# Moving a small side computation and its transfers from the projection part of a gated-DeltaNet stage into its matrix-inverse part

## The reference, cut to what matters

```
shift, scale, gate = split(c @ w_ada + b_ada, 3)          # modulate: w_ada is 1024 x 3072
h = x * (1 + scale) + shift

# gated_delta_rule, per head and chunk
lower = where(strict, (k*beta) @ k.T * decay, 0)
sol   = triangular_solve(lower + I, [v*beta | k*beta*exp(gc)])   # u and w
step:  v_new = u - w @ state;  o = qg @ state + qk @ v_new;  state = state*gl + kdec.T @ v_new
```

## Time and profile before

| | |
|---|---|
| median of 3 executions | 2713.7 us (2710.06 to 2719.28) |
| profiled execution, time | 2713.7 us |
| profiled execution, span of its instructions | 2711.8 us |
| mean granted TensorE clock | 0.971 of full |
| TensorE busy over the span | 93% |
| VectorE busy over the span | 37% |
| GpSimd busy over the span | 12% |
| `delta_stage` | about 1478 to 1940 us, turns of some 109 us |

### The profile page before, as it was taken

One profiled execution on the slowest core, in us unless ns is written; L12 is line 12 of the kernel. 1 busy time (PEld: TensorE's weight loads), 2 busy tenths in 40 slices (PEclk: granted clock), 3 DMA queues, 4 the chain that ended last, 5 costly groups with the idle time before them and its releaser, 6 DMA issues. The chain is left out here.

```text
span 2711.8 us, 37865 instructions
## 1 busy us (share of the span) xinstructions
PE 2525.0 (93%) x13849; PEld 1377.0 (51%) x13850; DVE 1005.6 (37%) x2302; ACT 672.4 (25%) x1468; POOL 337.3 (12%) x390
## 2 busy tenths in 40 slices
PE   6999999999999999999996999999899999899995
PEld 2665656656764443333332476685774434333332
DVE  2444344433543322322207535446343332222217
ACT  1031030310312222222222433443312222222221
POOL 0101001010001111111100212122101111111110
PEclk9999999999999999999997999999999999999998
DMA  7624326252628999999965211312437999999966
GB/s 281 191 63 146 102 92 189 61 164 66 224 101 322 365 421 420 411 413 413 407 250 215 78 50 59 97 54 66 163 131 290 345 420 420 399 414 411 404 264 276
DMA packets 177815, 654.93 MB, mean 242 GB/s; under 512 B 26884, under 2 KB 88684, under 8 KB 122504
## 3 DMA queue, kind: packets, MB, share of 16 engines
q1 hardware_dynamic: 112752, 394.89, 37.4%
q10 hardware_dynamic: 29784, 149.13, 14.4%
q0 software_dynamic: 35136, 109.10, 11.5%
HBM read 614.18 MB, written 53.52 MB: 246 GB/s over the span
## 5 line engine op out<-in xcount | busy, mean ns | idle before, releaser
L1462 DVE TENSOR_SCALAR core_oT<-moe_tx,moe_by,moe_plus 128x128 f32<-128x128 f32 x360 | 123.0, 404 | 661.6 <-PE moe_tx L1709 661.4
L675 PE MATMUL attn_proj<-core_hT,core_ring 128*128 128x512 f32 x768 | 334.4, 596 | 8.5 <-ACTq L497 5.1
L1734 PE MATMUL moe_ph<-weights_w,core_oT 128*32 128x512 f32 (+2 forms) x1216 | 307.4, 615 | 8.8 <-issue 8.7
L1748 PE MATMUL moe_py<-weights_w,moe_hT 128*32 128x512 f32 (+2 forms) x1296 | 312.8, 596 | 0.9 <-ACT moe_hT L1186 0.9
L1734 PE MATMUL moe_pr<-weights_w,core_oT 128*64 128x512 f32 (+2 forms) x864 | 276.6, 604 | 10.7 <-issue 9.7
L675 PEld LDWEIGHTS attn_proj<-core_hT,core_ring 128*128 128x128 f32 x768 | 146.5, 191 | 188.9 <-issue 183.2
L2392 PE MATMUL gdn_pj<-core_hT,core_ring 128*128 128x512 f32 x512 | 226.8, 597 | 0.0
L1269 POOL DMA_INDIRECT y_rows<-moe_ysb,moe_yidx x90 | 93.6, 1040 | 951.2 <-ACT moe_ysb L1199 726.1
L1186 ACT COPY moe_hT<-moe_th 128x256 f32<-128x256 f32 x90 | 33.6, 374 | 659.2 <-PE moe_th L1697 659.2
L671 PE MATMUL attn_proj<-core_ring,core_hT 128*128 128x256 f32 x768 | 176.5, 391 | 0.0
L671 PEld LDWEIGHTS attn_proj<-core_ring,core_hT 128*128 128x128 f32 x768 | 169.3, 282 | 11.2 <-issue 3.8
(11 more groups left out here) (410 smaller groups left out, 3433.6 us busy)
## 6 DMA issues: line engine op xcount, KB each, us to landing
weights_w<-in_expert_w_dram SPq DMA_DIRECT2D x160, 1024.0 KB
weights_w<-in_expert_w_dram ACTq DMA_DIRECT2D x92, 1024.0 KB
core_ring<-in_expert_w_dram SPq DMA_DIRECT2D x54, 1024.0 KB
core_hT<-in_expert_w_dram SPq DMA_DIRECT2D x48, 1024.0 KB
core_ring<-in_attn_w_in_dram SPq DMA_DIRECT2D x36, 1024.0 KB, 7.4
weights_w<-y_rows SPq DMA_DIRECT2D x32, 1024.0 KB, 13.1
core_ring<-in_expert_w_dram ACTq DMA_DIRECT2D x30, 1024.0 KB
attn_ada_w<-in_ada_w_dram POOLq DMA_DIRECT2D x64, 384.0 KB, 5.8
```

The costliest lines, as they stand in the source:

```text
L675: last = nc.tensor.matmul(proj[n % 2][:], w[:, j % SLOTS, kk, half_ * P:(half_ + 1) * P], c.hT[:, kk, :], start=kk == 0, stop=kk == KT - 1)
L1462: last = nc.vector.tensor_scalar(xT[:, b, k], tx[1][:, k - 4], by[:, k:k + 1], plus[:, k:k + 1], ALU.mult, ALU.add)
L1734: last = nc.tensor.matmul(ph[p % 2][at, :], xT[:, p % 2, k, at], w13[ew.up_place(n)[0]][:, :, k], start=k == 0, stop=k == KT - 1)
L1748: last = nc.tensor.matmul(py[n][at, :], hT2[:, p % 2, k, at], w2[ew.down_place(m)[0]][:, k, half(n)], start=k == 0, stop=k == 1)
```

## The change

Loads 2 to 5 are taken out of the early part of GpSimd's list and put behind the two products that make P0 (`P_ready`), ahead of the link matrices. Loads 6 and 7 are put between the link matrices of s = 0 and those of s = 1. All eight adds are taken out of the early part of VectorE's list. Adds 0 and 1 are put behind the E additions of step 0, adds 2 and 3 behind those of step 1, adds 4 and 5 behind step 2, adds 6 and 7 behind step 3. Numbers, sizes and buffers are as before.

```diff
@@ GpSimd's list
                 for h in range(HP):
-                    ada.load(pool, i, 2 + h)
                     pool.wait_ge(silu_ready, NCONV * i + h + 3)
                     pool.tensor_tensor(E1[h][:], kT[h][:], kT[h][:], ALU.mult).then_inc(kk_sq, 1)
                 for h in range(HP):
-                    ada.load(pool, i, 4 + h)
...
                 for h in range(HP):
-                    ada.load(pool, i, 6 + h)
...
                     pool.tensor_tensor(P0[h][:], M[h][:], over_t(masks[:, BELOW]), ALU.mult).then_inc(P_ready, 1)
+                for j in range(2, 6):
+                    ada.load(pool, i, j)
                 for s, dst in enumerate((P0, P1, P0)):
                     for h in range(HP):
...
                         pool.tensor_tensor(dst[h][:], M[h][:], over_t(masks[:, LINK + s]), ALU.mult).then_inc(n_ready[s], 1)
+                    if s == 0:
+                        ada.load(pool, i, 6), ada.load(pool, i, 7)
@@ VectorE's list
-                conv(0, K_), ada.add(dve, i, 0), conv(1, K_), ada.add(dve, i, 1), mask_causal(0), mask_causal(1)
-                conv(2, Q_), ada.add(dve, i, 2), conv(3, Q_), ada.add(dve, i, 3), conv(4, V_), ada.add(dve, i, 4)
-                norm_k(0), norm_k(1), ada.add(dve, i, 5), norm_q(0), norm_q(1)
-                keys(0), ada.add(dve, i, 6), keys(1), conv(5, V_), ada.add(dve, i, 7)
+                conv(0, K_), conv(1, K_), mask_causal(0), mask_causal(1)
+                conv(2, Q_), conv(3, Q_), conv(4, V_)
+                norm_k(0), norm_k(1), norm_q(0), norm_q(1)
+                keys(0), keys(1), conv(5, V_)
...
                         nc.vector.tensor_tensor(dst[h][:], ps[h][0][:], src[h][:], ALU.add).then_inc(e_ready[s], 1)
+                    if s < 4:
+                        ada.add(dve, i, 2 * s), ada.add(dve, i, 2 * s + 1)
```

## The result

The changed kernel takes 2744.18 us (median of 4, 2739.17 to 2751.66) against 2711.88 us (median of 4, 2706.49 to 2719.28): a ratio of 1.011, 95% interval 1.0086 to 1.0134. It is slower, by some 30 us. The forecast was 2739 us, range 2728 to 2752.

The account below looks back on a forecast made before the run. TensorE, busy for 93% of the span, was taken as the bound, with nil slack at step 2's E addition. Terms 3.0 + 1.55 + 0.7 + 1.1 = 6.3 us a turn, 25 over four turns: 2713.7 + 25 = 2739 us, range 2728 to 2752.

Parts of the forecast that it names:

- Nothing comes back from the projections: Projections: TensorE never waits for VectorE's adds there, so removing 7.7 us of them a turn gains 0 us.
- The E addition of step 2, 3.0 us: Inverse, head 0: adds 2 and 3 wait for slices ahead of this E addition, making TensorE's transpose 3.0 us late.
- GpSimd's queue, 1.55 us more: Inverse: loads 2 to 5 stand ahead of the first link matrices, adding 1.55 us, 4.55 us late in all.
- The third stall, 0.7 us for the link matrix behind load 7: Second link: loads 6 and 7 stand ahead of its link matrices, so TensorE waits 0.7 us more.
- The clock, 1.1 us net: Inverse: TensorE's gaps lower the granted clock, costing 1.1 us net a turn, between 0 and 2.6.
- Contention, left in the range: Inverse: adds 4 and 5 can overlap GpSimd's link matrices, delaying loads 6 and 7 by up to 0.6 us; not summed.
- adds 6 and 7 end by 1705.3: hidden: Inverse, after step 3: these adds end before the next E addition is wanted at 1706, so they cost nothing.
- The sum: Whole loop: 3.0 + 1.55 + 0.7 + 1.1 = 6.3 us a turn, 25 us over four turns.
- A: Inverse: the adds fit into VectorE's idle time, no change, 2713.7 to 2721 us; 1.7 us delay if slices had landed; chance 0.06.
- B: Projections: relief from the adds makes the kernel faster, at most 4 x 0.3 = 1.2 us; chance of real gain 0.02.
- C: Inverse: clock takes 2.6 us, with later landings and contention a turn costs 10.2 us, 2754 us; chance 0.17 for over 2746.

Follow-up runs that it names:

- the filled kernel: Changed kernel with five unread 128x512 products a turn added to TensorE, four before the E addition of step 2, one before the first link matrix: 117.45 us a turn, ratio 1.0126.
- only the second half was moved: Against the kernel before, only adds 4 to 7 and loads 6 and 7 moved to the change's places: 112.29 us a turn, ratio 1.0039.
- the four-buffer kernel with small link products: Changed kernel with four slice buffers, loads 2 and 3 early, and GpSimd's six link products a turn cut to one column: 110.73 us a turn, ratio 1.0014.
- the first experiment: Kernel before with the arithmetic of seven of a turn's eight adds left out, waits and counting kept: 109.09 us a turn, ratio 0.9999.
- the four-buffer kernel: Changed kernel with four slice buffers instead of two and loads 2 and 3 early in GpSimd's list: 115.74 us a turn, ratio 1.0103.

## Why the prediction was right, and where its terms were off

**Nothing comes back from the projections.** Right, and shown: windows of 62.0 us after, and 109.09 us a turn with the arithmetic of the adds gone.

**The E addition of step 2, 3.0 us.** Right in mechanism; it measured 3.6. The short term was the landing of the second slice of a pair. I took 3.4 us for every slice; load 2, issued at 1814.51, landed after 3.5 us, but load 3, issued 1.1 us later, after 4.2. The trace of the kernel before had this already: its loads 0 and 1 go out as a pair, and the second lands after 3.9 to 4.3 us. I had left them aside for those in mid-turn, which go out one by one. The fit cited from the Trainium skill (DMA: Bandwidth & Descriptors, section Anatomy of one DMA — SWDGE (gpsimd) path), an estimate of 2.9 us, is further off still.

**GpSimd's queue, 1.55 us more.** Right: 5.15 less 3.6 is 1.55, though after a slow transpose half of it shows as idle (0.85 us). The run with the link matrices ahead of loads 4 to 7 gave back 2.0 us, some of it contention's.

**The third stall, 0.7 us for the link matrix behind load 7.** Right only where the clock is kept up (0.93 us in the filled kernel). In the changed kernel the slow matmuls arrive after the link matrix.

**The clock, 1.1 us net.** The fall was right: 0.50 for 6.8 us in each turn. The Trainium skill (TensorE: Matmul & The Clock Gate, section HAM oscillation — how this bites in real kernels) and the trace agree that every turn has it. Its term stood in the sum as a cost of its own, and that was wrong: filling the gaps left the turn at 117.45. Nor is it zero by nature: the half-speed matmuls cost 1.65 and 2.7 us where no add was slowed, more than the 1.1 forecast.

**Contention, left in the range.** This is the term that was missing from the sum. I priced it from one add of 1.64 us and let it delay loads 6 and 7 by up to 0.6 us. It acted at another place. The adds in the third turn took 1.50 us in the mean:

```profile
L228 DVE SCALAR_TENSOR_TENSOR gdn_ada_acc<-gdn_ada_w,core_c,gdn_ada_acc 128x768 f32<-128x768 f32 x7 | 10.5, 1495 | 3.3 <-DMA gdn_ada_w<-in_ada_w_dram 3.1
```

and, against the step "adds 6 and 7 end by 1705.3: hidden", they end at 1834.75, which is 1709.3 on the old clock, and the E addition of step 4 waits for them. TensorE's lateness from this was 0.85 us in the changed kernel's third turn and 2.0 with the gaps filled; where only the second half was moved, TensorE waited 1.8 us there.

**The sum.** It was 6.3 us a turn and measured 8.35. By the third turn's lateness that is 3.6 for the E addition of step 2 (predicted 3.0), 1.55 for GpSimd's queue (1.55), 2.35 up to the products of link 1, all of it half-speed matmuls (1.8, made up of 0.7 for a link matrix and 1.1 for the clock), and 0.85 for the E addition of step 4 (nothing). This says where the lateness arose, and not what each cause would give back alone: the last two cover each other, as the filled gaps show. That the forecast of the third part comes near is partly luck, since one of its two terms was nil and the other too small. All that was left out made the turn longer, and the range had room for it.

**The rivals.** A, "it fits into the idle time", fell by 16.5 measured us of waits for VectorE. Its number for slices already there (1.7 us a turn) was met by the four-buffer kernel with small link products (1.64), and only by that one. B fell with the first experiment. C was right in that turns cost more than forecast, and that a second slice lands late, but its 2.6 us of clock is no cost to be added: filling the gaps gave nothing back. How much contention costs depends on how waits space the work: with four buffers the slice waits were gone and a turn was 1.7 us shorter; with the link products cut as well it was 6.7 us shorter.

## What to carry to other kernels

An engine's idle share says how much work fits, not where. Before moving work onto it, find the consumer that waits least (here 0.22 us between an E addition and its transpose) and ask what will stand in front of that addition in the same in-order queue, transfers' round trips included. Fixing one of two causes can show little when the other takes its place, so take both away once, and each alone. And fill or shrink a suspected loss before giving it a term: the half-speed matmuls were plain in the trace, and taking them away alone gained nothing, because another chain ended at the same point. A cut that removes two things at once (the link products' contention and their length) measures neither alone.

## What the runs showed of the hardware that was not expected

An add that reads two operands from SBUF (slice and accumulator) stood still beside GpSimd's products, and for more than one of them: 1.0 us alone, up to 4.7 us beside a row of four products that took 5.68. Beside link products, a slowed add ended 0.8 us after the end of one of them each time. In the same stretches the E additions, which read one operand from PSUM, took 0.69 us as always. The Trainium skill (SBUF — State Buffer, section SBUF: two separate sides) says that VectorE instructions with two SBUF inputs and GpSimd instructions that read SBUF exclude one another for a whole instruction. The runs agree on who is hit, and add that GpSimd's next products went ahead of the waiting add, up to three of them. One such add was recorded as begun 0.18 us before the first of these products and still came after the third. The products themselves took 1.26 to 1.30 us each, as alone; only the fourth of the row in the four-buffer kernel took 1.7 to 2.0, after an add had gone ahead of it. Why the add came in just there stays open.

The second of two 384 KB slices issued 1.1 us apart took 4.0 to 4.2 us to land in the changed kernel, where the first took 3.3 to 3.6 (once 4.1); issued 1.7 to 1.8 us apart, the second took 3.5 to 4.0.

Gaps of 3.26 to 3.46 us ahead of TensorE were followed, in each of the changed kernel's four turns, by 6.8 us at the granted clock 0.50; with four products in the gap whose result nobody reads it stayed at 1.00. The gap's length alone doesn't tell what follows: gaps of about 3.2 us with four buffers were followed by 3.4 us at 0.50, and one of 3.25 us in the kernel with the link matrices ahead of loads 4 to 7 by none; that turn was no shorter than its neighbours (115.39 us against 115.53 and 115.46).
